# Six projections of the second block made in one stage, with seven half-size products each and results by DRAM

## The reference

```python
h = rmsnorm(x, g[0])
proj = h @ w_in[l]
(mq, mk, mv, mo, mi, mf, dq, dk, dv, rq, rk, rv, rg, gates) = split_in(proj)
qk = jax.nn.silu(causal_dwconv(jnp.concatenate([mq, mk], axis=-1), mlstm_conv[l]))
hm = mlstm(mq_c, mk_c, mv, mi + bias_i, mf + bias_f)          # 4 heads of 256
hm = jax.nn.sigmoid(mo) * head_rms(hm)
hd = diff_attention(dq, dk, dv, lam)                          # 8 heads
hr = jax.nn.silu(rg) * head_rms(retention(rq, rk, rv))        # 4 heads of 256
gm, gd, gr = jnp.split(jax.nn.sigmoid(gates), 3, axis=-1)
y = gm * (hm @ w_mlstm_out) + gd * (hd @ w_diff_out) + gr * (hr @ w_ret_out)
```

## Time and profile before

| | us |
|---|---|
| median of 3 runs | 2375.13 |
| lowest, highest | 2374.03, 2375.13 |
| the profiled execution, its own time | 2375.63 |
| its span, first to last instruction | 2373.7 |
| TensorE busy | 2351.3 (99%) |
| VectorE busy | 1382.1 (58%) |
| ScalarE busy | 966.0 (41%) |
| GpSimd busy | 73.7 (3%) |
| stretch of the change (input gates to first differential head) | 1083.9 to 1737.9 |

### The profile page before, as it was taken

How to read it: one execution, slowest core, us unless ns; L and a number is a source line. 1 busy time by engine, 2 the same in 40 slices (tenths; PEclk the granted TensorE clock), 3 DMA queues, 4 the chain that set the end, 5 groups by cost and what they waited for, 6 DMA issues and landing times.

```text
span 2373.7 us, 29211 instructions
## 1 busy us (share of the span) xinstructions
PE 2351.3 (99%) x11396; PEld 1942.6 (82%) x11396; DVE 1382.1 (58%) x2143; ACT 966.0 (41%) x1731; POOL 73.7 (3%) x148
## 2 busy tenths in 40 slices
PE   8999999999999999999999999999999999999998
PEld 8778888888888888888888888888877888888887
DVE  4767876766768887776554222323356535564655
ACT  4444444424545444345444223322246534433323
POOL 3000000000000000000000000100000000000000
PEclk9999999999999999999999999999999999999999
DMA  4124324332212323323222332222322122323231
GB/s 144 50 78 126 125 87 142 101 113 89 72 54 89 107 92 103 119 90 112 71 88 72 107 100 77 72 88 89 93 73 71 54 89 98 98 72 124 88 124 71
DMA packets 177236, 220.23 MB, mean 93 GB/s; under 512 B 10031, under 2 KB 131084, under 8 KB 176864
## 3 DMA queue, kind: packets, MB, share of 16 engines
q1 hardware_dynamic: 173152, 204.82, 27.0%
q0 software_dynamic: 3968, 13.81, 1.9%
HBM read 216.48 MB, written 5.28 MB: 93 GB/s over the span
## 4 chain that ended last, share of the span: by engine, by line
PE 95%; DVE 3%; ACT 1%; issue 1%; DMA 0%; SPq 0%; DVEq 0%
PE B L590 45%; PE A L590 40%; PE C L590 7%; PE C L1052 1%; DVE ar L2319 0%; DVE WL L2110 0%; DMA X<-in_x 0%; PE C L1161 0%; PE C L1313 0%; DVE Y L2441 0%; DVE st L2422 0%; DVE XL L2266 0%; PE C L657 0%; PE C L876 0%; DVE X L2921 0%
## 5 line engine op out<-in xcount | busy, mean ns | idle before, releaser
L2110 DVE TENSOR_TENSOR WL<-RAW,WH 128x1024 fp32r<-128x1024 f32 (+3 forms) x346 | 395.6, 1184 | 384.3 <-ACT WH L1448 383.9
L590 PE MATMUL B<-XH,WH 128*128 128x512 f32 (+1 forms) x1432 | 542.7, 383 | 1.4 <-ACT XH L1505 0.8
L590 PE MATMUL B<-XH,WL 128*128 128x512 f32 (+1 forms) x1432 | 534.9, 378 | 0.0
L590 PE MATMUL B<-XL,WH 128*128 128x512 f32 (+1 forms) x1432 | 520.4, 379 | 2.9 <-DVE XL L2266 2.8
L1448 ACT ACTIVATE WH<-RAW 128x1024 fp32r<-128x1024 f32 (+4 forms) x362 | 353.0, 1025 | 406.4 <-PE A L590 266.2
L590 PEld LDWEIGHTS B<-XH,WH 128*128 128x128 f32 x1432 | 269.2, 188 | 68.3 <-issue 14.1
L590 PEld LDWEIGHTS B<-XH,WL 128*128 128x128 f32 x1432 | 269.3, 188 | 50.7
L590 PEld LDWEIGHTS B<-XL,WH 128*128 128x128 f32 x1432 | 260.4, 189 | 52.5 <-DVE XL L2266 4.6
L590 PE MATMUL A<-WH,XH 128*128 128x512 f32 (+2 forms) x688 | 260.6, 379 | 0.0
L590 PE MATMUL A<-WH,XL 128*128 128x512 f32 (+2 forms) x688 | 259.2, 377 | 0.0
L590 PE MATMUL A<-WL,XH 128*128 128x512 f32 (+2 forms) x688 | 259.1, 377 | 0.0
(11 more groups left out here) (368 smaller groups left out, 2948.2 us busy)
## 6 DMA issues: line engine op xcount, KB each, us to landing
RAW<-in_w_in SPq DMA_DIRECT2D x33, 1024.0 KB, 5.2
RAW<-in_mlp_w_up SPq DMA_DIRECT2D x32, 1024.0 KB, 5.4
RAW<-in_mlp_w_down SPq DMA_DIRECT2D x26, 1024.0 KB, 5.2
RAW<-in_w_in SPq DMA_DIRECT2D x48, 512.0 KB, 4.4
RAW<-in_w_ffn_in SPq DMA_DIRECT2D x22, 1024.0 KB, 5.1
RAW<-in_w_ffn_out SPq DMA_DIRECT2D x8, 1024.0 KB, 5.2
ar<-in_mlp_w_down SPq DMA_DIRECT2D x6, 1024.0 KB, 7.6
RAW<-in_mla_w_o SPq DMA_DIRECT2D x4, 1024.0 KB, 5.1
```

The source lines that it names most:

```text
L590: return nc.tensor.matmul(dst, l, r, start=first, stop=last)
L2110: x = tt(WL[s][:, part], RAW[s][:, part], f32(WH[s][:, part]), ALU.subtract)
```

## The change

Queries and keys of mlstm head 0 are made first (`ml0`). Then a new stage `xp` makes the six projections mv, rv, dv, mo, gates (the part for mlstm) and rg whole, one after another. Each is a product of 2 x 2 blocks (two halves of h's width by two halves of the output columns, and two halves of the tokens) made with seven block products of 24 matmuls. Four of the seven use sums of quarters of h, which are made once (`sum_one` to `sum_four` on VectorE, their high parts XS_H on ScalarE, low parts XS_L on VectorE; they live in YH and YL). Weight sums are made on VectorE (`weight_sum`, three for each projection, into RAW), but the last is made by a DMA of GpSimd's queue that adds 1 MB from DRAM onto the block in SBUF (`third_sum`, into XP_THIRD). ScalarE copies the first two results of a projection into quadrants of Y (`snapped`), VectorE combines the others there (`second_sum`, `upper_right`, `upper_left`, `with_fourth`, `lower_right`, `lower_left`, 1 of these without PSUM). ScalarE applies Sigmoid or Silu to mo, gates and rg in place (`functioned`). GpSimd's queue stores each quadrant (0.5 MB) to the DRAM tensor `projected`, and later reads from it the values (L_V), output gates (L_O) and mix gates (GATE_0, GATE) of each head, and F_V for `diff`.

Heads i now have only query and key chunks, and those of head i + 1 are made between scores and values of head i. `mix0` has only its four chunks of w_mlstm_out, and `dv` is gone. The work on the gates is spread: Exp at the end of projection 1, Ln, scans and the last Exp in projection 2. The load of the slopes (ALIBI) that waited for eight `mixed` still does, but `dv` no longer follows `mix1`. Semaphores are shared under new names (`rms_...`, `head_...`, `out_...`).

```diff
     ("pre", 0, 1, 0, 4, 0, 0),
     ("if", 1, 0, 2, 2, 0, 1),
-    ("ml", 16, 8, 24, 16, 4, 8),
-    ("mix0", 8, 4, 0, 0, 4, 0),
-    ("ret", 16, 8, 24, 16, 4, 8),
+    ("ml0", 2, 0, 4, 0, 0, 2),
+    ("xp", 42, 0, 0, 0, 0, 0),
+    ("ml", 8, 4, 24, 16, 0, 8),
+    ("mix0", 4, 2, 0, 0, 2, 0),
+    ("ret", 6, 4, 20, 16, 0, 6),
     ("mix1", 8, 4, 0, 0, 4, 0),
-    ("dv", 4, 2, 0, 0, 2, 0),
     ("diff", 10, 16, 0, 40, 0, 0),
...
+XP = ("mv", "rv", "dv", "mo", "gates", "rg")
+XP_AT = [BASE["xp"][0] + 7 * g for g in range(len(XP))]
+UNLOADED = {d + x for d in SEVEN_AT for x in (2, 3, 4, 6)} | {d + x for d in XP_AT for x in (2, 3, 5, 6)}
...
+    "ml": (("ml", 1, "q"), ("ml", 1, "k"), ("ml", 0, "v"), ("ml", 2, "q"), ("ml", 2, "k"), ("ml", 1, "v"),
+           ("ml", 3, "q"), ("ml", 3, "k"), ("ml", 2, "v"), ("ret", 0, "q"), ("ml", 3, "v"), ("ret", 0, "k")),
+    "ret": (("ret", 1, "q"), ("ret", 1, "k"), ("ret", 0, "v"), ("ret", 2, "q"), ("ret", 2, "k"), ("ret", 1, "v"),
+            ("ret", 3, "q"), ("ret", 3, "k"), ("ret", 2, "v"), ("ret", 3, "v")),
...
+        def project(g):
+
+            d = XP_AT[g]
+            for q, (hs, ls, k0, at) in enumerate((
+                    (XH, XL, 0, 0), (XS_H, XS_L, 0, 0), (XS_H, XS_L, 0, 256), (XS_H, XS_L, 0, 768),
+                    (XH, XL, 4, 0), (XH, XL, 4, 256), (XS_H, XS_L, 0, 512))):
+                n, of = 7 * g + q, xp_banks(g, q)
...
+                    else:
+                        pe.wait_ge(*xp_read(n - 4, x))
+                    for j in range(4):
+                        lhs = slice(at + P * x, at + P * x + P)
...
-        def mlstm_head(i, ahead, first=False):
-
-            c = c0 + 4 * i
-            features(c + 1, slot(c0 + 1), XH, XL, rb // 2 + 3 * i + 1)
-            if first:
-                gates_by_token()
-            for j in range(2):
-                tokens(c + 2 + j, slot(c0 + 2 + j), XH, XL, 4 * j, 4, 512, ra + 2 * i, j == 0, j == 1)
+        def mlstm_scores(i):
 
             pe.wait_ge(s_("ml_qk"), 4 * i + 4)
-            scores("ml", i, ra + 2 * i + 1, L_Q, L_K)
...
+        mlstm_scores(0)
+        pe.wait_ge(s_("xp_dve"), 13 * len(XP))
+        gates_by_token()
+        for i in range(3):
+            if i:
+                mlstm_scores(i)
+            head_features("ml", i + 1, "q")
+            if i:
+                head_transposed("ml", i - 1, L_H)
+            head_features("ml", i + 1, "k")
...
+            third_high(d + 3)
+            if g == 0:
+                sums_high(3, 768)
+            snapped(g, 1, 0, 1)
+            split(d + 4)
+            if g == 0:
+                sums_high(4, 512)
+            elif g == 1:
+                after_conv(0, 1)
+            elif g == 2:
+                act.wait_ge(s_("if_act"), 1)
+                nc.scalar.activation(G_L, G_L, ACT.Ln, bias=1.0).then_inc(s_("if_act"), 1)
+            sum_high(g, d + 5, other, 4)
+            functioned(g, 0)
+            act.wait_ge(s_("xp_more"), 16 * g + 16)
+            third_high(d + 6)
+            functioned(g, 1)
...
-        split(BASE["ml"][0] + 1)
-        dve.wait_ge(s_("if_l"), 1)
-
...
+        def gate_logs():
+
+            dve.wait_ge(s_("if_act"), 2)
+            then(stt(G_F, G_F, 0.0, G_L, ALU.min, ALU.subtract))
+            then(nc.vector.tensor_tensor_scan(G_B, G_F, G_0, 0.0, ALU.add, ALU.add))
+
+        def gate_maxima():
+
+            dve.wait_ge(b_free[0], BASE["if"][2] // 2 + 1)
+            then(tt(G_U, G_I, G_B, ALU.subtract))
+            then(nc.vector.tensor_tensor_scan(G_M, G_U, G_U, 0.0, ALU.max, ALU.max))
+            tt(G_EM, G_B, G_M, ALU.add).then_inc(s_("if_dve"), 1)
 
...
+            weight_sum(g, XP_THIRD)
+            if g == 0:
+                sum_four()
+            low_both(d + 2, other)
+            if g:
+                lower_left(g - 1)
+            if g == 1:
+                convolution(0, 1, 0)
+            elif g == 2:
+                gate_logs()
+            low_both(d + 3, XP_THIRD)
+            if g == 0:
+                sums_low(3, 768)
+                sum_three()
+            second_sum(g)
+            split(d + 4)
+            if g == 0:
+                sums_low(4, 512)
+            elif g == 1:
+                convolution(0, 1, 1)
+            elif g == 2:
+                gate_maxima()
+            dve.wait_ge(lo_ready, d + 3)
+            weight_sum(g, raw)
+            upper_right(g)
+            low_both(d + 5, other)
+            upper_left(g)
+            low_both(d + 6, XP_THIRD)
+            if g == 1:
+                dve.wait_ge(b_free[1], BASE["if"][2] // 2 + 1)
+                stt(G_T, G_F, -1.0, G_F, ALU.mult, ALU.max).then_inc(s_("if_dve"), 1)
+            with_fourth(g)
+            split(d + 7)
+            if g + 1 < len(XP):
+                project_weights(g + 1)
+
+        project_weights(0)
+        for g in range(len(XP)):
...
+        c0, ra, _, _, g0, _ = BASE["mix0"]
+        split(c0 + 1)
+        head_lo("ml", 3)
+        for h in range(2):
+            for kh in range(2):
+                if 2 * h + kh < 3:
+                    split(c0 + 2 * h + kh + 2)
+            dve.wait_ge(s_("gate_in%d" % h), 16)
+            for t in range(T):
+                wait_tok(dve, t, g0 + h, c0 + 2 * h + 1)
+                tt(Y[:, t, 512 * h:512 * h + 512], (GATE_0, GATE)[h][:, t, :], A[t][:], ALU.mult).then_inc(a_free[t], 1)
...
+        def third_sum(g):
+
+            d, at = XP_AT[g], OFF[XP[g]] + 512
+            pool.wait_ge(lo_ready, d + 4)
+            pool.dma_start(grid(XP_THIRD, 4, 512), a["w_in_2"][0].rearrange("(k p) n -> p k n", p=P)[:, 0:4, at:at + 512],
+                           accum_op=ALU.add).then_inc(s_("xp_more"), 16)
...
+        for g in range(len(XP)):
+            if g:
+                project_out(g - 1, (2, 3))
+            third_sum(g)
+            project_out(g, (0, 1))
...
+        pool.dma_start(F_V, scratch("dv")).then_inc(s_("lv_in"), 16)
         pool.wait_ge(s_("mixed"), 8)
-        pool.dma_start(ALIBI, a["c_alibi"]).then_inc(s_("alibi_in"), 16)
+        pool.dma_start(ALIBI, a["c_alibi"]).then_inc(s_("decay_in"), 16)
```

More of the change, by code:

```diff
@@ new lines, in _, with head_rms @@
+        for g in range(len(XP)):
+            project(g)
+        functioned(len(XP) - 1, 2)
+        functioned(len(XP) - 1, 3)
+        def head_rms(name, i, inv):
+            for t in range(T):
+                bank, free, n = head_bank(name, i, t)
+                if inv:
+                    act.wait_ge(s_(name + "_d"), T * i + t + 1)
+                    nc.scalar.activation(L_H[:, t, :], bank[:, 0:256], ACT.Copy, scale=stat(H_INV + t)).then_inc(free, 1)
+                else:
+                    act.wait_ge(s_("head_o"), T * nth(name, i) + t + 1)
+                    copy(L_H[:, t, :], bank[:, 0:256]).then_inc(free, 1)
+                act.wait_ge(free, n + 1)
+                nc.scalar.activation(xtmp[:, t // 2, 256 * (t % 2):256 * (t % 2) + 256], L_H[:, t, :], ACT.Square, scale=256 ** -0.5,
+                                     accum_out=stat(H_SS + t)).then_inc(s_("head_ss"), 1)
@@ L1864, in mix @@
+            if i < 3:
+                before_conv(i + 1, 1)
+                after_conv(i + 1, 1)
+            head_rms("ml", i, True)
+        for i in range(4):
+            mlstm_head(i)
+        retention_part(0, 1)
+        c0 = BASE["mix0"][0]
+        split(c0 + 1)
+        head_hi("ml", 3)
+        for c in range(c0 + 2, c0 + 5):
+            split(c)
         def mix(name, split_to):
@@ L1912, in diff_split @@
             split(c)
[L1914 to L1923 removed]
+        mix("mix1", 2)
         c0, ra, rb, n0, _, f0 = BASE["diff"]
@@ L2760, in retention_head @@
[L2760 to L2777 removed]
+                dve.wait_ge(s_("head_s"), T * nth("ret", i) + j + 1)
@@ new lines, in retention_head @@
+                tt(L_A[:, j, 0:n], A[j][:, 0:n], DECAY[:, i, 0:n], ALU.mult).then_inc(a_free[j], 1)
+            if i < 3:
+                retention_part(i + 1, 0)
+                split(QK_AT["ret", i + 1, "k"] + 1)
+            if i:
+                head_lo("ret", i - 1)
+            if i < 3:
+                retention_part(i + 1, 1)
+            values_by_token("ret", i)
+        for i in range(4):
+            retention_head(i)
+        split(BASE["mix1"][0] + 2)
+        head_lo("ret", 3)
@@ new lines, in _ @@
+        project_out(len(XP) - 1, (2, 3))
+        all_out()
+        pool.wait_ge(lo_ready, XP_AT[-1] + 7)
+        load_out_gates("mo", 0)
+        pool.wait_ge(s_("if_t"), 2)
+        load_values("mv", 0)
+        for i in range(4):
+            head_rms("ml", i)
+            if i < 3:
+                load_values("mv", i + 1)
+                pool.wait_ge(s_("head_h"), T * i + T)
+                load_out_gates("mo", i + 1)
+        load_values("rv", 0)
+        pool.dma_start(GATE_0, scratch("gates")[:, :, 0:512]).then_inc(s_("gate_in0"), 16)
@@ new lines, in _ @@
+        pool.dma_start(DECAY, a["c_decay"]).then_inc(s_("decay_in"), 16)
+        pool.wait_ge(s_("head_t"), 8)
```

(10 more changed lines are left out.)

728 lines of the change are left out of this document (442 added, 286 removed).

## The result

| | before | after |
|---|---|---|
| median, us | 2375.13 | 2387.06 |
| lowest, highest, 5 runs each | 2374.03, 2375.35 | 2382.06, 2387.94 |
| the profiled execution, its own time | 2375.63 | 2382.06 |
| its span | 2373.7 | 2380.2 |
| TensorE busy | 2351.3 | 2326.5 |

The ratio of the medians is 1.0048, 95% interval 1.0037 to 1.006: slower by half a per cent. The forecast was 2381.6 with a range of 2368 to 2397. The span of the profiled execution grew by 6.5 us, which is the forecast to a tenth. The median grew by 11.9, and the profiled execution is the fastest of the five. Both facts need an explanation, and so does the agreement, since several of its terms were off.

What follows compares the result with a forecast made beforehand. The prediction took TensorE, busy 99% of the span, to bound the kernel. Matmuls saved -32.6, products on summed operands +1.2 and waits +37.9 gave +6.5 us on 2375.1, so 2381.6 us, range 2368 to 2397.

Steps and rivals of the forecast that it cites:

- products on sums: In the projections, 24 products on summed operands take TensorE 0.05 us more each: +1.2 us.
- projections 4 and 5: Sigmoid and store of the projection before delay second_sum's writing of the quadrant: 0.6 us each, 1.2 together.
- mlstm heads: Scores of heads 1 to 3 wait for the convolution and Silu chain, convolutions at 3.2: 8.6 us together.
- into retention head 0: Key features of retention head 0 wait for bank B until head_rms has read it: 0.7 us.
- Part 2: Six projections: VectorE's fixed order makes TensorE wait, including 8.6 us in projection 2 behind Ln and scan; sixth-product cover 0.65.
- part 4: In mix0, chunk 2 waits for VectorE's evictions, now behind the low part of chunk 3: 4.3 us.
- part 1: Input gates to first differential head: matmuls of 128x512 fall from 2496 to 2352, saving 32.6 us.
- gate_maxima: In projection 2 it stands on VectorE before a weight sum without cover and costs TensorE 2.7 us.
- part 5: SP's loads, stores and read-backs of values, and the slopes' load should cost nothing; slopes 2.9 us at most without cover.
- A: Rival: the projections' accumulating DMA lands late, beyond 11.9 us; at 14.5 it costs 9.6 us, giving 2391; chance 0.17.
- B: Rival: VectorE is not late in the projections, cover at product 5 over 3.1; 10 us less, 2371.6; chance 0.2.
- C: Rival: the projections' 0.5 MB stores to DRAM land late; at 6.0 us, 1.6 a projection, giving 2391; chance 0.13.

Runs made afterwards that it cites:

- Experiment 4: Kernel before, with only mix0's first-half evictions put behind the low part of a chunk that needs the end of the evicted chunk: 2381.46 us, ratio 1.0026.
- experiment 5: Changed kernel with gates' work and mix0 evictions moved, its accumulating DMA turned into a plain load, one addition left out: 2374.05 us, ratio 0.9996.
- experiment 7: Changed kernel with mix0 evictions moved and two waits shortened; second key convolution and gates' work moved behind product 5's combination: 2362.72 us, ratio 0.9951.

## Why the prediction was right, and where it was not

The direction and the mechanism were right: the matmuls saved are outweighed by waits that the new order brings. The size came out for the profiled execution, but by luck in good part, as the balance of that execution shows, in us:

| term | forecast | measured (idle + 0.27 each) |
|---|---|---|
| matmuls taken out | -32.6 | -32.6 (144 fewer) |
| products on sums | +1.2 | 0: their distance is 0.2265 as that of others |
| projection 0 and its start | 5.3 | 5.0 |
| projection 1 | 3.2 | 3.4 |
| projection 2 | 11.3 | 10.3 |
| projections 4 and 5 | 1.2 | 0 |
| end of projections | 2.1 | 2.6 |
| mlstm heads | 8.6 | 5.7 |
| into retention head 0 | 0.7 | 2.4, at another place |
| mix0 | 4.3 | 4.6 |
| retention | 1.2 | 3.0 |
| low clock | none | 3.8 |

The waits sum to 37.0 against 37.9, by luck in part: 5.1 too much in projections 2, 4 and 5 and the heads stand against 3.5 too little on the way into retention and in it. The 1.2 for products on sums were too much as well, and the low clock, that the sum didn't have, made up for them. To the waits come 3.8 of low clock in the changed kernel, and 1.5 are to be taken off, since the trace of before had one low stretch that the one of after hadn't: the window from 1070 to 1080, before,

```profile
1070.00:1080.00 10.00, 8.63 (x49) 0.83 0.27 84
```

That makes -32.6 + 37.0 + 3.8 - 1.5 = 6.7, and 6.5 were measured. The changed kernel's trace is 0.3 ahead already at 1061, before all this.

**Right.** Part 2's chain for projection 2 (8.6 forecast, 8.47 idle and 0.16 measured), part 4's price for mix0 (4.3 and 4.29), and that the sixth product has hardly any cover. The 2352 matmuls of part 1 are right too, by its 10 + 4 + 6 + 8 chunks; its parenthesis "14 less than" does not lead there. The accumulate landed in 8.7 us (forecast 10.6 from two passes) and was hidden.

**Priced too high in part 2.** gate_maxima was to come out whole, 2.7. The wait at the sixth product of projection 2 is 0.57, with its restart 0.8. The 0.6 each in projections 4 and 5 didn't come at all.

**Nearly right: part 5.** No wait of TensorE names a load of SP, a store or the slopes. Two small costs came even so where the prediction had put nothing. The first is behind another engine: the first products of projections 1 and 2 wait 0.22 and 0.41 for a low part, and its high part began late, since ScalarE waited for SP's load up to 8.1 us. With restarts this is 1.2 us, in the rows of those projections. Waits of ScalarE after, 1104 to 1355:

```profile
ACT WH L1597 <- DMA RAW<-in_w_in: 27.7, 5, 8.1
```

The second is the read-back of the values of retention head 3, 0.9 us with its restart and in the row of retention:

```profile
1641.33 1.56 PE L694 MATMUL B<-ar 128*128 128x256 f32 x6 [0.63 <-DMA ar<-projected]
```

GpSimd issued it at 1637.32, behind its work for the head before: 4.0 us ahead of its use, and not over 20.

**Mis-sized: the heads.** Three waits of 0.82, 1.10 and 1.11 on ScalarE's Silu, not 2.6 to 3.0. The mis-sized term is the convolution's 3.2, taken from the loop of before. In the changed kernel the heads are written out, and the four operations follow each other at 0.03 us, not 0.15. Timeline of VectorE after:

```profile
1406.43 0.49 DVE L2910 TENSOR_SCALAR ar<-ar,vec 128x512 f32<-128x512 f32 x1 [4.61 <-ACT ar L1934]
1406.95 0.75 DVE L2911 SCALAR_TENSOR_TENSOR ar<-ar,vec 128x512 f32<-128x512 f32 x1
1407.74 0.75 DVE L2912 SCALAR_TENSOR_TENSOR ar<-ar,vec 128x512 f32<-128x512 f32 x1
1408.53 0.75 DVE L2913 SCALAR_TENSOR_TENSOR ar<-ar,vec 128x512 f32<-128x512 f32 x1
```

It takes 2.85 in place of 3.2, and three of them stand in the chain: 1.0 us each time. The trace of before had both prices: head 0's query convolution is written out there, and its operations start at 1098.77, 1099.29, 1100.07 and 1100.86, 0.03 apart, while those of the earlier trace rows are in the loop. The prediction read the change of the loop in the order, but kept the price of the loop. Partly in place of this came three waits of 0.35 on the copy of bank B, between the head's features and its values, that the sum didn't have.

**Mis-placed.** The way into retention head 0: I priced bank B for its key features. The trace shows TensorE waiting 2.12 for VectorE's low part of head 2's output in bank C before the values of head 3. I had seen that this work stands behind a chunk's high and low parts in the chain of the heads, and not asked the same for head 3, where no key features lie between transposes and values.

**Missing: the clock, and with it, as far as the record shows, 5 us of the median.** The step that failed is in the first paragraph, "every wait that the new order puts before TensorE is a loss at once": it is more than that. The sum priced each wait at its length. Measured are its length, 0.27 for the restart, and in a part of the cases a stretch at the lower clock that costs 1.4 to 2.4. Experiment 4 gives 6.3 for a wait of 4.3. Twenty-three waits, five of them above 2 us, gave 3.8 us of low clock in the profiled execution. In the median one it must be about 9, if the 5 us between the two are all clock; no trace shows that one. The trace of before has hardly a wait in the middle, but its one low stretch there, from 1070 on, stands right behind the wait of 2.1 on VectorE. It was there to be read, and I didn't ask what was ahead of it.

**The table load.** The page "ScalarE: Activation LUTs" of the Trainium skill (section "Table sets: the hidden batching unit") has ln and exp in one set. The trace after has the load of 1.28 us before the Ln, so the measurement decides against it here, at least as this program is built.

**The rivals.** A is ruled out by experiment 5. B is ruled out for the order as it stood (2.10 at the place named), but its idea, that VectorE has idle time enough, is what experiment 7 uses. C: the stores took 5.6 us, near the upper bound of 6.0, and cost nothing, where the prediction had priced 6.0 at 1.6 a projection. VectorE waited for one only once, for 0.6 us, in the changed kernel's projections, and TensorE never did.

What stays open is why the same wait of 2.1 us brings a low clock in one execution and not in another. No experiment here varies the length of a wait alone.

## What to carry to other kernels

When a change takes work from the engine that bounds a kernel, its gain is known and its price is the new waits. Put them together one by one from the order in which the other engines do their work, and look at what stands ahead of each operation that the bounding engine needs. Follow such a chain through the other engines to the DMA behind it, since the wait of the bounding engine names only its last link. Give inserted work a place where its engine is idle in the trace, not a place of the same number of operations: here order and finer waits alone decided some 24 us. And price a wait of TensorE above its length, since the clock behind it can be low.
